# First mixer begun before its shift is known, modulation tiles redistributed, and layer 1's output begun inside the recurrence's end, in one inference step of a two-layer hybrid trunk

## The reference, cut to what matters

```python
def modulation(cvec, w_mod, b_mod):
    m = jax.nn.silu(cvec) @ w_mod + b_mod
    return jnp.split(m[:, None, :], 6, axis=-1)

def adaln(x, g, shift, scale):
    return rmsnorm(x, g) * (1 + scale) + shift

def mixer_ab(h, w_in, w_out, ...):                       # layer 0
    z = h @ w_in
    za = jax.nn.gelu(z[..., :2 * A_DIM])
    u, v = za[..., :A_DIM], za[..., A_DIM:]
    v = layernorm(v, v_g, v_b)
    v = einsum over chunks with ws, plus bs
    ya = u * v
    zb = z[..., 2 * A_DIM:]
    glu = zb[..., :B_DIM] * jax.nn.sigmoid(zb[..., B_DIM:])
    yb = jax.nn.silu(rmsnorm(dwconv(glu, conv_w, conv_b), norm_g))      # 31 taps
    return jnp.concatenate([ya, yb], -1) @ w_out

def rwkv_time_mix(...):                                  # layer 1, one half of the heads
    y_f, kd_f, s_f = direction(0, s0_f, False)
    y_b, kd_b, s_b = direction(1, s0_b, True)
    y = y_f + y_b
    yc = y - mean(y)
    yn = yc * lax.rsqrt(mean(yc * yc) + GN_EPS) * ln_g + ln_b
    bonus = jnp.sum(r * (kd_f + kd_b) * r_k, -1) * v
    out = (yn + bonus) * g

def mixer_cd(...):
    out = jnp.concatenate([yc, yd], -1) @ w_out          # yd: attention

xc = xc + mc[2] * oc                                     # residual, then a gated ConvFFN in every layer
```

## Time and profile before

| | |
|---|---|
| median of 3 runs | 1999.68 us (1998.92 to 2001.86) |
| the profiled execution | 2000.47 us |
| its span in the profile | 1998.6 us |
| TensorE busy / VectorE busy | 94% / 53% of the span |

### The profile page before, as it was taken

One profiled execution on the slowest core, in us unless ns is written; L12 is line 12 of the kernel. 1 busy time (PEld: TensorE's weight loads), 2 busy tenths in 40 slices (PEclk: granted clock), 3 DMA queues, 4 the chain that ended last, 5 costly groups with the idle time before them and its releaser, 6 DMA issues.

```text
span 1998.6 us, 43869 instructions
## 1 busy us (share of the span) xinstructions
PE 1884.6 (94%) x18252; PEld 1730.5 (87%) x18252; DVE 1061.9 (53%) x1864; ACT 768.8 (38%) x1216; POOL 598.1 (30%) x327
## 2 busy tenths in 40 slices
PE   6899899999999998999998998989799999999996
PEld 3765699999999998878877887878699999999996
DVE  4497755442144547947566666666455443144423
ACT  4111335552155435237454232323144553145521
POOL 2300153444244445211111111111044444344442
PEclk8999899999999999899998999999899999999998
DMA  8666332222122221120110000000022222122221
GB/s 346 269 263 231 133 131 80 74 81 73 67 73 73 89 69 42 51 75 33 43 60 2 3 3 3 3 3 3 7 74 74 73 73 87 61 74 73 81 77 62
DMA packets 35344, 159.67 MB, mean 80 GB/s; under 512 B 3936, under 2 KB 4448, under 8 KB 28560
## 3 DMA queue, kind: packets, MB, share of 16 engines
q1 hardware_dynamic: 32832, 152.02, 20.9%
q10 hardware_dynamic: 1872, 3.61, 0.5%
q0 software_dynamic: 512, 2.13, 0.3%
HBM read 154.73 MB, written 3.01 MB: 79 GB/s over the span
## 4 chain that ended last, share of the span: by engine, by line
PE 83%; DVE 7%; ACT 3%; issue 3%; POOL 2%; DMA 2%; SPq 0%; DVEq 0%; PEldq 0%; POOLq 0%; ACTq 0%; PEld 0%
PE ps L220 18%; PE ps L222 18%; PE ps L221 18%; PE ps L1931 10%; PE ps L1970 2%; PE ps L706 2%; PE ps L696 2%; PE ps L1910 2%; PE ps L366 2%; DMA arena<-in_mod_w 2%; PE ps L1506 1%; PE ps L1227 1%; PE ps L1508 1%; PE ps L1507 1%; PE ps L2054 1%
## 5 line engine op out<-in xcount | busy, mean ns | idle before, releaser
L259 POOL TENSOR_TENSOR w_lo<-wslot,w_hi 128x1024 fp32r<-128x1024 f32 x130 | 319.7, 2460 | 690.5 <-ACT w_hi L254 690.5
L220 PE MATMUL ps<-xa_hi,w_hi 128*128 128x322 f32 (+1 forms) x1440 | 446.1, 310 | 0.0
L222 PE MATMUL ps<-xa_hi,w_lo 128*128 128x322 f32 (+1 forms) x1440 | 446.0, 310 | 0.0
L221 PE MATMUL ps<-xa_lo,w_hi 128*128 128x322 f32 (+1 forms) x1440 | 444.9, 309 | 0.0
L220 PEld LDWEIGHTS ps<-xa_hi,w_hi 128*128 128x128 f32 x1440 | 271.8, 189 | 0.2
L254 ACT ACTIVATE w_hi<-wslot 128x1024 fp32r<-128x1024 f32 x130 | 138.1, 1062 | 347.2 <-PE ps L222 289.8
L221 PEld LDWEIGHTS ps<-xa_lo,w_hi 128*128 128x128 f32 x1440 | 271.3, 188 | 0.2
L222 PEld LDWEIGHTS ps<-xa_hi,w_lo 128*128 128x128 f32 x1440 | 271.2, 188 | 0.0
L1931 PE MATMUL ps<-arena 64*64 64x64 f32 (+2 forms) x5760 | 243.3, 238 | 15.0 <-DVE arena L2238 12.6
L1931 PEld LDWEIGHTS ps<-arena 64*64 64x64 f32 x5760 | 214.5, 136 | 31.4 <-DVE arena L2238 16.7
L220 PE MATMUL ps<-hid_hi,d_hi 128*128 128x320 f32 x704 | 218.0, 310 | 3.9 <-POOL hid_lo L1106 3.9
(11 more groups left out here) (214 smaller groups left out, 3315.8 us busy)
## 6 DMA issues: line engine op xcount, KB each, us to landing
arena<-in_mod_w SPq DMA_DIRECT2D x48, 1024.0 KB, 7.1
wslot<-in_ffn_up SPq DMA_DIRECT2D x88, 512.0 KB, 3.5
wslot<-in_ffn_down SPq DMA_DIRECT2D x32, 704.0 KB, 4.0
wslot<-in_cd_w SPq DMA_DIRECT2D x22, 512.0 KB, 3.5
wslot<-in_w_out SPq DMA_DIRECT2D x16, 512.0 KB, 3.5
wslot<-in_ab_w SPq DMA_DIRECT2D x12, 512.0 KB, 8.1
x<-in_x_fm SPq DMA_DIRECT2D x2, 1280.0 KB, 7.3
out_y<-arena ACTq DMA_DIRECT2D x8, 320.0 KB, 2.4
```

The source lines that it names most:

```text
L220: nc.tensor.matmul(out, wh[:, m], hi[:, kk, t], start=(kk == 0), stop=False)
L221: nc.tensor.matmul(out, wh[:, m], lo[:, kk, t], start=False, stop=False)
L222: last = nc.tensor.matmul(out, wl[:, m], hi[:, kk, t], start=False, stop=(kk == k_all - 1))
L259: pool.tensor_tensor(wl[:, :], wslot[:, s, 0:tile_cols[base]], wh[:, :], ALU.subtract).then_inc(lo_ready, 1)
```

## The change

**First mixer.** The scale's four tiles come first (`j ^ TURN`), and VectorE makes h = x * amul * rs in one instruction per chunk and token group, without the shift. TensorE takes tile 0's tokens chunk by chunk with modulation tiles 4 to 7 between them, then tile 1's second half; the shift is multiplied as two extra columns (24 matmuls of 2 columns), and is added to the products of later tiles where they are read (`gate_of_glu`, `gated`). ScalarE adds the shift to h before the v tiles. **Modulation tiles**: one per glu tile instead of two, three per v tile instead of two, two or three per u tile, tiles 40 and 41 ahead of the output, 42 and 43 between its halves; the `mod_dve` steps stand later among the taps. **Value branch's root** is put ahead of the u tiles' gelu. Low parts of the mixed chunks are made between the mixes. **Recurrence's end**: the gate rounds come before the last outputs; ScalarE and GpSimd make weight and source parts of seven chunks while VectorE finishes the eighth, whose steps are folded: bonus and bias times gate ahead of the reciprocal, then one product and one add. Rows of layer 1's w_out are turned, so that the last pair's chunk is the last in the product. One of the two meetings of all engines (`pass_gate`) goes.

```diff
-            sp.dma_start(mod_slot(j), io["mod_w"][j].rearrange("p (k q c) -> p k q c", k=2, q=TURN)).then_inc(mod_arrival(j)[0], 16)
+            sp.dma_start(mod_slot(j), io["mod_w"][j ^ TURN if j < 2 * TURN else j].rearrange("p (k q c) -> p k q c", k=2, q=TURN)).then_inc(mod_arrival(j)[0], 16)
...
-            layer, i = turn // TURNS, turn % TURNS
+            layer, i = turn // TURNS, turn % TURNS if turn >= 2 else 1 - turn
...
-            mod(*range(FIRST_TILES))
+            mod(0, 1, 2)
             tile(0)
+            mod(3)
             tile(1)
+            mod(4, 5, 6, 7)
             for name, dst in (("ws_t", wsT), ("v_rows", vrow), ("bs_rows", bsg)):
                 sp.dma_start(dst, io[name]).then_inc(loaded, 16)
             mod(8, 9, 10)
             for n in range(2, GLU_TILES):
                 tile(n)
-                mod(2 * n + 7, 2 * n + 8)
+                mod(n + 9)
...
-            mod(*range(25, 37))
+            mod(*range(18, 35))
             tile(10)
+            mod(35, 36)
+            tile(11)
             mod(37, 38)
-            tile(11)
-            mod(39, 40)
             tile(12)
-            mod(41)
+            mod(39, 40, 41)
             tile(13)
...
+            def first_tiles():
+                base = ab["glu"]
+                take_parts(pe, base, 0, 0)
+                for kk in range(KD):
+                    chunk_of_h(pe, 0)(kk)
+                    product_of_parts(base, 0, [kk], KD, xa_hi, xa_lo, XA_TOKENS)
+                    if 3 <= kk < 7:
+                        mod_pe(pe, kk + 1)
+                take_parts(pe, base, 0, 1)
+                product_of_parts(base, 1, range(4), KD, xa_hi, xa_lo, XA_SECOND)
+                mod_columns_pe(pe, 1)
+                product_of_parts(base, 1, range(4, KD), KD, xa_hi, xa_lo, XA_SECOND)
+                pe.wait_ge(shift_ready, 1)
+                product_of_parts(base, 0, range(KD), KD, xa_hi, xa_lo, XA_SHIFTS).then_inc(product, 1)
+                product_of_parts(base, 1, range(KD), KD, xa_hi, xa_lo, XA_FIRST).then_inc(product, 1)
+                mod_pe(pe, 8, 9)
...
+            first_tiles()
+            for n in range(2, GLU_TILES):
                 glu_tile(n)
-                if n % 2 == 0 and n:
-                    mod_columns_pe(pe, n // 2 + 1)
-                mod_pe(pe, 8 + 2 * n, 9 + 2 * n)
+                if n == 4:
+                    mod_columns_pe(pe, 2)
+                mod_pe(pe, 8 + n)
...
+            pe.wait_ge(h_full, KD)
             for t in range(NT):
...
                 v_tile(t)
-                if t % 2 == 0:
-                    mod_columns_pe(pe, 5 + t // 2)
-                mod_pe(pe, 24 + 2 * t, 25 + 2 * t)
-            for n, js in enumerate(((34, 35), (36, 37), (38,), (39,))):
+                if t != 1:
+                    mod_columns_pe(pe, 3 + t - (t > 1))
+                mod_pe(pe, 16 + 3 * t, 17 + 3 * t, 18 + 3 * t)
+            for n, js in enumerate(((31, 32), (33, 34), (35, 36), (37, 38, 39))):
                 u_tile(n)
-                if n == 1:
-                    mod_columns_pe(pe, 8)
+                if n in (1, 3):
+                    mod_columns_pe(pe, 7 + n // 2)
                 mod_pe(pe, *js)
             pe.wait_ge(vmul_ready, NT)
...
             mix(3)
+            mod_pe(pe, 40, 41)
             pe.wait_ge(mix_used, 3)
             out_part(0, range(KA), True)
             pe.wait_ge(mix_used, 4)
             out_part(1, range(KA), False)
-            mod_pe(pe, 40, 41, 42, 43)
+            mod_pe(pe, 42, 43)
             out_part(0, range(KA, KD), True)
...
+                if i == 1:
+                    mod_act(act, 2)
+                if i < 2:
+                    act.wait_ge(src_lo["pool"], BY_POOL)
+                    act.wait_ge(src_lo["dve"], KD - BY_POOL)
+                    for k in range(4 * i, 4 * i + 4):
+                        add_shift(k)
             warm(act, ACT.Gelu_apprx_tanh)
             for t in range(NT):
+                if t != 1:
+                    mod_act(act, 3 + t - (t > 1))
                 gelu_of_v(t)
-                if t % 2:
-                    mod_act(act, 6 + t // 2)
             squares_of_conv(0)
-            gelu_of_u(0)
-            mod_act(act, 8)
-            gelu_of_u(1)
             act.wait_ge(var_ready, 1)
             nc.scalar.activation(lnmv[:, :, 1], lnmv[:, :, 1], ACT.Sqrt, bias=eps_c[:, 0:1]).then_inc(std_ready, 1)
             warm(act, ACT.Gelu_apprx_tanh)
+            gelu_of_u(0)
+            mod_act(act, 7)
+            gelu_of_u(1)
             gelu_of_u(2)
...
             gated(1)
-            mod_dve(dve, st, 2)
             after_low_part_of(5)
             first_tap(1)
             taps(3, {0: 14, 1: 1})
             after_low_part_of(6)
             taps(4, {0: 17, 1: 4})
             gated(2)
...
-            mod_dve(dve, st, 3)
+            mod_dve(dve, st, 2)
...
             gated(3)
-            mod_dve(dve, st, 4)
...
             first_tap(3)
             taps(2, {0: 29, 1: 16})
             taps(4, {1: 18, 2: 1, 3: 1})
-            mod_dve(dve, st, 5)
+            mod_dve(dve, st, 3)
...
+                if g:
+                    y_lo_of(g - 1)
+            mod_dve(dve, st, 8)
             mod_dve(dve, st, 9)
-            for k in range(KA):
-                dve.wait_ge(ya_ready, k + 1)
-            source_lo(dve, "dve", KD, ycat, y_hi, y_lo, range(KA))
+            y_lo_of(KA - 1)
...
             need((LAST, "RM", 2))
             for r in range(ROUNDS):
                 chain(LAST, r)
+            for g in range(2):
+                round_of((END, "gate", g), scan_w[:, HP - 1, 2 * P:3 * P], lg)
             outputs(LAST)
             wait(y_read, len(UNITS))
             for g in range(2):
...
             wait(tail_sq, HP)
             for g in range(2):
                 round_of((END, "var", g), head_ones, rkv[:, HP - 1, :])
-            for g in range(2):
-                round_of((END, "gate", g), scan_w[:, HP - 1, 2 * P:3 * P], lg)
+            wait(emptied["act"], entry[END, "var", 1][2])
+            wait(emptied["dve"], entry[END, "mean", 1][2])
...
+            wait(emptied["dve"], entry[LAST, "RM", 2][2])
+            tile_hi(act, cd["out"], 0, 0)
+            tile_hi(act, cd["out"], 0, 1)
+            for n in range(KD - 1):
+                nc.scalar.activation(y1_hi[:, n, :], ycat1[:, Y1_OF[n], :], ACT.Copy).then_inc(src_hi, 1)
+            for g in range(2):
+                take_bank((END, "gate", g), half(last_gate, g), half_bank((END, "gate", g)))
             tail_square(END, HP - 1)
             tail_root(END)
+            act.wait_ge(last_y, 1)
+            nc.scalar.activation(y1_hi[:, KD - 1, :], ycat1[:, Y1_OF[KD - 1], :], ACT.Copy).then_inc(src_hi, 1)
...
+            y, bonus = ycat1[:, HP - 1, :], rkv[:, KA + HP - 1, :]
+            wait(emptied["act"], entry[END, "gate", 1][2])
+            wait(emptied["dve"], entry[LAST, "bonus", 1][2])
+            wait(emptied["dve"], entry[END, "mean", 1][2])
+            st(nc.vector.scalar_tensor_tensor(out=bonus, in0=bonus, scalar=pcol("ln_b", HP - 1), in1=last_gate, op0=ALU.add, op1=ALU.mult))
+            st.wait()
+            st(nc.vector.scalar_tensor_tensor(out=last_gate, in0=y, scalar=pcol("ln_g", HP - 1), in1=last_gate, op0=ALU.mult, op1=ALU.mult))
             for part in range(4):
                 tail_root(END, part)
-            tail_norm(END, HP - 1)
-            tail_affine(HP - 1)
-            tail_add(HP - 1)
-            tail_gate(END, HP - 1)
+            st.wait()
+            wait(tail_sq, HP)
+            st(nc.vector.tensor_tensor(y, last_gate, rs[:, :], ALU.mult))
+            st.wait()
+            nc.vector.tensor_tensor(y, y, bonus, ALU.add).then_inc(last_y, 1)
...
             wait(step_read, STEPS_READ * len(UNITS))
             pool.dma_start(io["new_state"], fins).then_inc(fin_out, 16)
+            tile_lo(pool, cd["out"], 0, 0)
+            for n in range(KD - 1):
+                pool.wait_ge(src_hi, 3 * KD + n + 1)
+                pool.tensor_tensor(y1_lo[:, n, :], ycat1[:, Y1_OF[n], :], y1_hi[:, n, :], ALU.subtract).then_inc(src_lo["pool"], 1)
             pool.wait_ge(fin_out, 16)
+            pool.wait_ge(last_y, 1)
+            tile_lo(pool, cd["out"], 0, 1)
...
-            mod_pe(pe, *range(FIRST_TILES))
+            mod_pe(pe, 0, 1, 2, 3)
             mod_columns_pe(pe, 0)
-            mod_columns_pe(pe, 1)
             ab_pe(pe)
...
+            tile_hi(act, ab["glu"], 0, 0)
             mod_act(act, 0)
+            for k in range(KD):
+                act.wait_ge(h0_ready, k + 1)
+                nc.scalar.activation(xa_hi[:, k, 2:XA], h[:, k, :], ACT.Copy).then_inc(src_hi, 1)
+                if k == 4:
+                    tile_hi(act, ab["glu"], 0, 1)
...
-            for k in range(KD):
-                normed_dve(dve, st, k)
             dve.wait_ge(par_in, 16)
             mod_dve(dve, st, 0)
+            for k in range(KD):
```

(28 more changed lines are left out.)

101 lines of the change are left out of this document (61 added, 40 removed).

## The result

The changed kernel takes 2004.24 us (median of 20 runs, 2002.12 to 2008.19), the kernel before 1999.66 (20 runs beside them, 1996.51 to 2002.92). The ratio is 1.0026 [1.002, 1.0032]: slower by 4.6 us, just beyond what can be told from no change. The forecast was +2.3 us (2002.0), and the measured time lies inside its range; the chance went mostly to "no change that can be told" (0.40), then to slower (0.35).

A forecast was written before the change was run, and what follows sets the result against it. The prediction took TensorE to bound the kernel, with VectorE second in the first mixer. Early stage +10.9 less tail 8.6 gave +2.3 us on the median 1999.68, so 2002.0, range 1992 to 2010.

The forecast's parts named there:

- First product: Start of first mixer: h some 10 us sooner, last low part near 45, end near 61.5; gain 1.2 us.
- rival A: First mixer: VectorE's whole chain moves forward, so new waits on it do not form; 1992 to 1993; chance 0.22.
- Next weight tiles: SyncE's queue: weight tiles come some 10 us later, three products each wait 0.6 to 0.8 more; +2.0 us.
- Modulation tiles: First mixer, tiles spread: TensorE waits at product 5, net +2.7 us, and at tile 20 for mod_dve(3), +4.5.
- the early stage: Everything before the recurrence: a loss of +10.9 us, to be paid whole; bounds +6 and +14.
- Mixing: Mixing and output's first half: waits for squares and at tile 40 cost 14.0 us, 11.1 goes; net +2.9.
- Tail: End of the recurrence: output starts early, last chunk done at 1453.0 against 1461.6; gain 8.6 us, bounds 6 and 10.2.
- the sum for the last chunk: Recurrence's end: reciprocals from 1442.4, product, add, low part held by GpSimd until 1452.0, six matmuls, done at 1453.0.
- The gate rounds themselves: Recurrence's end: gate rounds ahead of the last outputs, 1.59 us, 0.4 of it in the present wait; +1.3.
- a sign of being wrong: TensorE's clock: the prediction is wrong if it stays high where the prediction has it low.
- Rival B: First mixer: more VectorE taps meet weight low parts, 2.2 us each; three more give +8.9, 2008.5; chance 0.25.

The follow-up runs named there:

- the run with step 3 sooner: Changed kernel with mod_dve(3) moved ahead of twelve of the sixteen taps between the bias step and it: 2006.26 us, ratio 1.0043 to the kernel before.
- tile 13 alone: Changed kernel with w_out tile 13 put ahead of modulation tiles 40 and 41 in SyncE's order: 1998.09 us, ratio 0.9987 to the kernel before.
- the tail alone: Kernel before with only the change's end of the recurrence, first mixer as before: 1997.97 us, ratio 0.999.
- long gaps between them: Changed kernel with a 640-column memset on GpSimd ahead of subtractions 3 and 4: 1997.82 us in a single execution.
- GpSimd first: Changed kernel with GpSimd's output parts ahead of its last-chain wait and state DMA, second weight low part beside the reciprocals: 1995.32 us, ratio 0.9972 to before.

## Why the prediction came out as it did

*First product: right in its time, and in part by luck.* First h at 26.0, as forecast, its last low part at 43.7 (45); tiles 8 and 9 used at 60.97 (61.5); gain 1.7 for 1.2. The clock was not as forecast: the last chunks, put at the low level, ran at the high one (0.31 at 46.67; granted 1.00, 2.4 GHz, from 46.4 to 49.2), and the other half of the second tile, put at the high one, in part at the low (0.47 at 54.87; granted 0.50, 1.2 GHz, from 54.7 to 57.9), behind the 24 matmuls of two columns, which with 2.6 us took longer than forecast too. TensorE had to do the rest of its work there, and the 12 us of the early start are not kept: rival A's condition, a whole VectorE chain moved forward, did not come.

*Next weight tiles: right.* Tile 2 was issued at 48.0 (47 to 50); the waits are 0, 0.64 and 1.82, 2.5 for 2.0.

*Modulation tiles: right, each a little smaller.* Product 5 waits 4.82 (6.3 forecast) and begins at the low level (granted 0.50 from 93.4 to 99.0), as forecast; tile 20 waits 2.74 (3.6). That VectorE's chain doesn't move was the step that carried the early stage; gated(1), bias step and step 3 are within 0.8 us of before. What I had not seen is that the wait at tile 20 is only the first of a row of such places (tile 24 behind it): mending one pays nothing, as the run with step 3 sooner showed.

*Mixing: right.* Squares 4.21 and tile 40 4.62 (4.6 and 5.3). Sum of the early stage: +10.4 by the trace, +10.9 forecast. Two of the terms were tested apart: tile 13 alone is worth 6.8 to 7.8 us (4.6 + 2.2 forecast), step 3 nothing by itself.

*Tail: mis-sized.* 8.6 was forecast, with bounds of 6 and 10.2; 3.3 came by the trace, 3.1 with the tail alone. The step that failed: the sum for the last chunk has no term for the two instructions with the gate that were put ahead of the reciprocals. Between the roots (1441.8) and the reciprocals (1442.4) it leaves 0.6 us, though it lets GpSimd's subtractions run beside them until 1445.4; the turns that it priced there were those of the reciprocals, which were not held. The runs showed 7.82 instead of 0.9 for the first of the two: VectorE got no turn, and the reciprocals began at 1455.99, 6.0 after the roots were there for TensorE (1449.97). With GpSimd's subtractions done sooner, or long gaps between them, the hold was gone. The last low part behind GpSimd's weight (2.35) was as forecast.

The clock moved two more terms. The roots came some 2.4 us sooner than forecast, counted from the state's DMA: the products of mean and variance took 1.34 each (1445.32; granted 1.00 from 1445.3 to 1449.4), where before they took twice as long, granted 0.55 from 1433.3 to 1441:

```profile
1433.31 2.50 PE L1910 MATMUL ps<-arena,const 128*128 128x320 f32 x4 [0.92 <-DVE arena L2269]
```

In the runs with the tail alone and with GpSimd first, where the gate rounds also stand ahead of the last outputs, they took 1.34 too. The gate rounds themselves, put at +1.3 (1.59 less 0.4 is rather 1.2), took 2.40. And the 21 matmuls behind the long wait, six of them of the first product, ran at the low level (0.27 us apart, granted 0.50 from 1465.1 to 1470.8), where I had the high one: 2.5 us lost. That the seven chunks ran at the high level (42 matmuls in 6.4, not 8.5) gave nothing, since TensorE waits behind them in any case. The prediction named a clock that stays high where it had it low as a sign of being wrong; that sign came, here and in the first product.

*Total.* +10.4 - 3.3 = +7.1 by the two traces, +4.6 by the medians; the forecast's +2.3 was right in its sign because the early loss is larger than the tail's gain in either case. That the time lies so near the forecast is luck in part: the tail missed by 5.3 us, and about half of that went in the difference between traces and medians. Rival B came without its price: three taps met low parts (2.91 at 81.54, 2.64 at 89.31, and one of the eight at 100.01, 8.73 together against 6.59 before), where one did before, but VectorE had its 8.34 us wait shortened to 2.78 in exchange, and gated(1) and the bias step did not move. None of the rivals had what made the tail small, the held bonus instruction.

What stays open: the 2.5 us between the difference of the two profiled executions and that of the medians, which no row places.

## What to carry to other kernels

When work is moved to an engine that was idle, ask what it will share, and whether it will pause: that two engines took turns in one place doesn't promise that they do in another. An instruction much longer than its twin, with no idle time ahead of it, is read against what its neighbour engine runs at the same time. And a first stage begun 12 us sooner is worth only what the next chain can use: here VectorE's taps set the pace, so the change to keep was the tail's, with GpSimd's work put first, in the old first mixer.
